# Chunk places laid out anew and a new TensorE order in the mixers of a two-layer mixer and mixture-of-experts step on one core

## What is computed

```python
for l in range(2):
    sh1, sc1, g1, sh2, sc2, g2 = split(silu(cond) @ w_ada[l] + b_ada[l], 6)   # per group of tokens
    h = rms_norm(x, norm1_g[l]) * (1 + sc1) + sh1
    z = h @ w_in[l]                       # 1024 -> 2048 mixer columns + 4 * 1024 gate logits
    # four mixers on the 2048 columns: conv (31 taps, layer norm, silu), Fourier,
    # windowed attention with rotary embedding and sinks, 2-D neighbourhood attention
    proj = einsum('blnc,ncd->blnd', branches, w_branch[l])
    merged = einsum('blnd,blnd->bld', sigmoid(gate_logits), proj)
    x = x + g1 * (merged @ w_out[l])
    h = rms_norm(x, norm2_g[l]) * (1 + sc2) + sh2
    aff = softmax(h @ w_router[l])        # 16 experts; each takes its top tokens (16 prompt, 32 sample)
    x = x + g2 * scatter_add(expert_swiglu(h[idx]) * g)
y = rms_norm(x, final_norm_g)
```

## Time and profile before

| what | us |
|---|---|
| median of 3 runs | 1682.55 (1682.27 to 1686.41) |
| the profiled execution's own time | 1680.36 |
| its span | 1678.5 |
| TensorE matmuls busy | 1558.4 (93%) |
| DVE, ACT, POOL busy | 522.1, 493.8, 358.9 |
| DMA | 536.72 MB, mean 320 GB/s |

### The profile page before, as it was taken

One profiled execution on the slowest core, in us unless ns is written; L12 is line 12 of the kernel. 1 busy time (PEld: TensorE's weight loads), 2 busy tenths in 40 slices (PEclk: granted clock), 3 DMA queues, 4 the chain that ended last, 5 costly groups with the idle time before them and its releaser, 6 DMA issues.

```text
span 1678.5 us, 20053 instructions
## 1 busy us (share of the span) xinstructions
PE 1558.4 (93%) x8363; PEld 955.6 (57%) x8363; DVE 522.1 (31%) x864; ACT 493.8 (29%) x910; POOL 358.9 (21%) x196
## 2 busy tenths in 40 slices
PE   7999999999999998799799999999999998988986
PEld 4988889984333343242279888899733433423322
DVE  3733453533121121121157234445411211212013
ACT  4435454433112021121153455534321211211212
POOL 1544455730000000000035444558000000000000
PEclk9999999999999999999999999999999999999999
DMA  9624444479999999999994434445799999999995
GB/s 377 243 100 152 160 151 151 149 304 418 428 426 426 427 426 427 427 428 428 421 392 158 138 124 151 151 158 221 327 422 426 428 426 428 427 426 428 426 427 237
DMA packets 52098, 536.72 MB, mean 320 GB/s; under 512 B 13584, under 2 KB 13992, under 8 KB 20008
## 3 DMA queue, kind: packets, MB, share of 16 engines
q1 hardware_dynamic: 52008, 535.43, 77.7%
HBM read 533.05 MB, written 2.36 MB: 319 GB/s over the span
## 4 chain that ended last, share of the span: by engine, by line
PE 68%; DMA 22%; ACT 4%; DVE 3%; issue 1%; POOL 1%; SPq 0%; DVEq 0%; ACTq 0%
PE psum L967 22%; PE psum L1771 17%; DMA ring<-in_w_e_down 11%; PE psum L1800 8%; DMA ring<-in_w_e_gu 8%; PE psum L1200 4%; PE psum L1130 3%; PE psum L1739 3%; PE psum L1817 2%; PE psum L707 2%; DMA ring<-in_w_in 1%; DMA ring<-in_w_ada 1%; PE psum L1103 1%; PE psum L1082 1%; ACT WSR L1220 1%
## 5 line engine op out<-in xcount | busy, mean ns | idle before, releaser
L967 PE MATMUL psum<-HTH,WSR 128*128 128x384 f32 x1536 | 412.3, 342 | 1.8 <-ACT arena L630 1.6
L1771 PE MATMUL psum<-ring,arena 128*64 128x512 f32 x1504 | 339.7, 596 | 27.9 <-DMA ring<-in_w_e_gu 26.6
L967 PEld LDWEIGHTS psum<-HTH,WSR 128*128 128x128 f32 x1536 | 280.4, 188 | 14.9 <-issue 11.8
L899 POOL TENSOR_TENSOR WSR<-ring,WSR 128x1024 fp32r<-128x1024 f32 x92 | 224.0, 2434 | 252.5 <-ACT WSR L1220 252.5
L967 PE MATMUL psum<-HTL,WSR 128*128 128x384 f32 x768 | 259.4, 338 | 0.0
L1771 PEld LDWEIGHTS psum<-ring,arena 128*64 128x64 f32 x1504 | 103.5, 137 | 232.8 <-issue 186.7
L1948 DVE TENSOR_TENSOR arena<-arena,psum 64x512 f32<-64x512 f32 x64 | 44.1, 690 | 503.1 <-PE psum L1771 315.0
L1800 PE MATMUL psum<-ring,arena 128*64 128x512 f32 x864 | 193.5, 595 | 5.2 <-DMA ring<-in_w_e_down 5.2
L1220 ACT ACTIVATE WSR<-ring 128x1024 fp32r<-128x1024 f32 x96 | 101.6, 1059 | 281.8 <-PE psum L967 279.4
L967 PEld LDWEIGHTS psum<-HTL,WSR 128*128 128x128 f32 x768 | 144.8, 189 | 1.0 <-issue 1.0
L1854 ACT ACTIVATE arena<-psum 64x512 f32<-64x512 f32 x64 | 37.7, 589 | 347.9 <-PE psum L1771 347.7
(11 more groups left out here) (221 smaller groups left out, 1695.1 us busy)
## 6 DMA issues: line engine op xcount, KB each, us to landing
ring<-in_w_e_gu SPq DMA_DIRECT2D x94, 2048.0 KB, 31.2
ring<-in_w_e_down SPq DMA_DIRECT2D x54, 2048.0 KB, 31.4
ring<-in_w_ada SPq DMA_DIRECT2D x24, 2048.0 KB, 10.7
ring<-in_w_in SPq DMA_DIRECT2D x22, 2048.0 KB, 7.9
arena<-in_w_e_gu SPq DMA_DIRECT2D x22, 1536.0 KB, 29.1
arena<-in_w_e_gu SPq DMA_DIRECT2D x12, 2048.0 KB, 29.5
arena<-in_w_e_down SPq DMA_DIRECT2D x10, 2048.0 KB, 31.4
C<-in_w_e_gu SPq DMA_DIRECT2D x22, 512.0 KB, 30.8
```

What stands on the lines that cost most here:

```text
L899: nc.gpsimd.tensor_tensor(WSR[:, 1, i % 2], part_src(i), WSR[:, 0, i % 2].bitcast(F32), ALU.subtract).then_inc(S["w_rest"], 1)
L967: ins = nc.tensor.matmul(ps[:, 0:TOK], WSR[:, w, i % 2, k, :], x[:, k, :], start=(k == 0 and w == 0 and x is HTH), stop=(k == KT - 1 and w ...
L1771: ins = nc.tensor.matmul(pb[half][64 * m:64 * m + 64, :], XE[:, k, j, :], w[:, half * CH:(half + 1) * CH], start=(k == 0), stop=(k == KT - 1))
```

## The change

1. **Mixer order.** fa2 comes behind the projection cq1. rot0 and rot1 come behind dq0, rotk behind zcv, lt0 and lt1 behind that, lt2 behind dk0, lb0 and lb1 behind dv0, ko behind dv1. vt0 to vt2 come inside gate step 0, behind its gate tile. ACT's order follows, with the square root behind the copy of dk1.
2. **Modulation.** ADA_AT changes from {0: 4, 4: 5, 8: 6, 11: 7, 20: 8, 24: 9} to {2: 4, 5: 5, 8: 6, 11: 7, 14: 8, 17: 9, 20: 10}: chunk 10 is multiplied at step 20 and kept in bank 4 until the routing. Chunk 11 is multiplied where chunk 10 was, behind the last logits. ada4, 8, 9 and 10 are loaded into slot 6.
3. **Places.** The order is now 4, 0 (after w_branch), LOW, HIGH, 1, 6, 2, 3, 5. Chunk 0 is fetched when the last attention output is copied. Chunk 9 (ONCE) has a place of its own, half in GROW, half in once_slot, used once a layer. The chunks after it turn through the nine places as before.
4. **What makes room.** The split of the merged rows (MRGH) moves from ring slot 4 to XN, laid out by token tile; the last branch's rest (BRL_LAST) to ring slot 5; an expert's transposed activations from AT into XE; one square's output into the arena.
5. **Banks.** wo{t}_{half} has bank (t + 3 half) mod 4; rt{t} keeps bank t; ada10 has bank 4.

```diff
-        ADA_AT = {0: 4, 4: 5, 8: 6, 11: 7, 20: 8, 24: 9}
+        ADA_AT = {2: 4, 5: 5, 8: 6, 11: 7, 14: 8, 17: 9, 20: 10}
...
-                 "w5", "ada7", "w8", "wb23", "w9", "ada8", "w10", "ada9", "w11", "wo0", "wo1", "ada10", "ada11"]
+                 "w5", "ada8", "ada7", "w8", "wb23", "ada9", "w9", "w10", "ada10", "w11", "wo0", "wo1", "ada11"]
...
-        MRGH = over("MRGH", "ring", 4 * 4 * D, KT * TOK)[:, :].rearrange("p (k t) -> p k t", k=KT)
+        MRGH = over("MRGH", "XN", 0, KT * TOK)[:, :].rearrange("p (t k n) -> p k t n", t=TT, k=KT)
...
-                T.add(f"wo{t}_{half}", 2 * t + half)
+                T.add(f"wo{t}_{half}", (t + half * TT) % 4)
...
-            PLACE = (LOW, HIGH, unit_at["wo0"][0], SPARE, unit_at["wo1"][0], 3, 4, unit_at["ada10"][0], unit_at["ada11"][0])
+            third = 3 - unit_at["wo0"][0] - unit_at["wo1"][0]
+            PLACE = (4, third, LOW, HIGH, unit_at["wo0"][0], SPARE, unit_at["wo1"][0], 3, unit_at["ada11"][0])
             RING = len(PLACE)
+            ONCE = RING
+            def turn(x):
+                return x if x < ONCE else x - 1
...
-                s, landing = PLACE[x % RING], e_land[x % RING]
+                if x == ONCE:
+                    sp.dma_start(GROW[:, 0].rearrange("p i d -> p (i d)"), src[:, 0:2 * D]).then_inc(once_land, 16)
+                    sp.dma_start(once_slot, src[:, 2 * D:4 * D]).then_inc(once_land, 16)
+                    return
+                s, landing = PLACE[turn(x) % RING], e_land[turn(x) % RING]
...
+                    if s == 4:
+                        copied(sp, f"o{len(ATT) - 1}")
...
+                    elif name == "w11":
+                        first_chunk(0)
                     elif name == "wo1":
-                        first_chunk(0)
-                sp.wait_ge(S["out_kv"], base("out_kv") + 64)
-                for x in range(1, RING - 1):
+                        first_chunk(1)
+                        sp.wait_ge(S["out_kv"], base("out_kv") + 64)
+                        first_chunk(2)
+                for x in range(3, RING - 1):
                     first_chunk(x)
...
                 used_up(sp, "ada11")
                 fetch(sp, RING - 1, chunk(l, (RING - 1) // PER, (RING - 1) % PER))
+                sp.wait_ge(S["x_mixed"], base("x_mixed") + 2 * TT)
+                sp.wait_ge(S["router_exp"], base("router_exp") + 1)
+                fetch(sp, ONCE, chunk(l, ONCE // PER, ONCE % PER))
...
-                for x in range(RING, NE * PER):
-                    used_place_of(x - RING)
+                for x in range(ONCE + 1, NE * PER):
+                    used_place_of(x - RING - 1 if x < 2 * RING + 1 else x - RING)
...
-                ada_main(pe, l, 10)
+                ada_main(pe, l, 11)
```

More of the change, by code:

```diff
@@ L976, in mixer_tensor, with channel_dft @@
                     copied(pe, f"zf{c}")
-                for t in range(TT):
+                def channel_dft(t):
                     ps = open_tile(pe, f"fa{t}")
@@ new lines, in rotated, with conv_rows @@
+                def rotated(n, src):
+                    ps = open_tile(pe, n)
+                    close_tile(nc.tensor.matmul(ps[:, 0:DEC], rot, src, start=True, stop=True), n)
+                def conv_rows(t):
+                    ps = open_tile(pe, f"lt{t}")
+                    a0 = 0 if t == 0 else USAMP - PADC + (t - 1) * P
+                    for c in range(2):
+                        ins = nc.tensor.transpose(ps[:, c * P:(c + 1) * P], ACC[:, c, a0:a0 + P], ident)
+                    close_tile(ins, f"lt{t}")
@@ new lines, in normed_back, with prompt_keys @@
+                def normed_back(c):
+                    ps = open_tile(pe, f"lb{c}")
+                    for t in range(TT):
+                        ins = nc.tensor.transpose(ps[:, t * P:(t + 1) * P], LNX[:, t, c * P:(c + 1) * P], ident)
+                    close_tile(ins, f"lb{c}")
+                def prompt_keys():
+                    ps = open_tile(pe, "ko")
+                    for n in ("cq0", "cq1", "ck", "dk0", "dk1"):
+                        copied(pe, n)
+                    for c, src in enumerate((KTC[:, 0:P], DK[:, 0, 0:P], DK[:, 1, 0:P])):
+                        ins = nc.tensor.transpose(ps[:, c * P:(c + 1) * P], src, ident)
+                    close_tile(ins, "ko")
@@ L983, in mixer_tensor, with value_rows @@
+                def value_rows(t):
+                    ps = open_tile(pe, f"vt{t}")
+                    for c in range(3):
+                        ins = nc.tensor.transpose(ps[:, c * P:(c + 1) * P], VT[:, c, t * P:(t + 1) * P], ident)
+                    close_tile(ins, f"vt{t}")
+                channel_dft(0)
+                channel_dft(1)
                 zt("cq1")
+                channel_dft(2)
                 ps = open_tile(pe, "ctxT")
@@ L1044, in att_scores @@
+                zt("dk0")
+                conv_rows(2)
+                zt("dk1")
+                zt("dv0")
+                for t in range(TT):
+                    copied(pe, f"lt{t}")
+                for c in range(2):
+                    normed_back(c)
+                zt("dv1")
+                prompt_keys()
                 def att_scores(g):
@@ L1118, in mixer_tensor @@
                         zt(f"g{n}_{k}")
+                        if idx == 0:
+                            for x in ("zcv", "dv0", "dv1"):
+                                copied(pe, x)
+                            for t in range(TT):
+                                value_rows(t)
                         if go is not None:
@@ L1331, in mixer_scalar @@
                     if idx == 0:
-                        for c in range(2):
-                            ps = take(act, f"lb{c}")
-                            release(nc.scalar.activation(BRT[:, 0, c, :], ps[:, 0:TOK], ACT.Silu, scale=PRM[:, 128 + c:129 + c],
-                                                         bias=PRM[:, 130 + c:131 + c]), f"lb{c}")
+                        for t in range(TT):
+                            copy_out(f"vt{t}", ZV[:, t, :], lambda ps: ps[:, 0:384])
                     if go is not None:
```

181 lines of the change are left out of this document (86 added, 95 removed).

## The result

The changed kernel took 1677.05 us (median of 10 runs, 1669.57 to 1680.45), the kernel before 1684.95 in the runs beside it. The ratio is **0.9947, interval 0.9929 to 0.9965**: 0.5% faster, by the ratio 8.9 us, where 23 were forecast. The profiled execution took 1675.76 us (span 1674.0), 4.6 less than that of before.

A forecast was written before the change was run, and what follows sets the result against it. TensorE was taken to bound the mixer and the DMA stream the experts. Places -6.4 and order -5.1 gave -11.5 us a layer, -23.0 for two, hence 1659 us; forecast 1653 to 1665, range with rivals 1650 to 1670.

The forecast's parts named there:

- Order ahead of step 7: TensorE's reordered mixer up to step 7's gate tile: forecast 6.5 us less a layer.
- -0.9: Channel DFT: a projection now covers the third tile's 0.92 us wait for ACT, 0.9 us less a layer.
- -3.8: Mixer transposes put between projections: -4.4 us, plus 0.6 for a new wait, so 3.8 us less a layer.
- the softmax wait of 1.78: Attention: TensorE's wait for the first scores' softmax goes, covered by moved modulation chunk 4.
- The new wait for the normalised rows: Behind dv0, TensorE waits for rows scaled after ACT's square root: +0.6 us, between 0 and 2.
- Chunk 10's +1.9 less the second softmax wait: Modulation chunk 10 added to the attention steps costs 1.9 us; the fifth scores' 1.49 us wait goes.
- w4: w_in piece loaded one step later, some 3.5 us after ACT wants it; covered, so 0, up to 3.5 us.
- rival (b): Order gains nothing: late w4, square root and ACT's table loads eat it; only the places count, 1670 us, chance 0.12.
- The logits on the last w_out tile's bank: Routing: tile 1's logits wait for DVE to empty the bank shared with the last w_out tile, +1.0 us.
- The places: Expert chunks: more loaded early and chunk 9's own place end the stream 6.4 us earlier a layer, bounds 4.9 to 8.1.
- the lag of 1.4 us: Start lag of the emptied DMA engines, read at one start; used for restarts instead of the skill's 2.0.
- The clock: Rival: TensorE stays at 1.2 GHz over a whole first expert group, 1817 us, chance 0.03; short dip 1.7 a layer.

The follow-up runs named there:

- c2: b3 with modulation chunk 4 multiplied at step 0 again, as in the kernel before: 1662.34 us, ratio 0.9863 to the kernel before.
- a1: Changed kernel with modulation chunk 5 multiplied at step 4 instead of 5, so w4 loads earlier: 1666.93 us, ratio 0.9888 to the kernel before.
- a4: Changed kernel with the chunk places of the kernel before, leaving the new order alone: 1687.86 us, ratio 1.0013 to the kernel before.
- b1: Changed kernel without the place used once; chunk 9 takes the first ring place again: 1683.65 us, ratio 1.0005 to the kernel before.
- a3: Changed kernel with chunk 5 at step 4 and tile 1's logits in PSUM bank 5: 1663.87 us, ratio 0.9869 to the kernel before.
- b3: b2 with two of six groups of logits moved into w_out tiles: 1658.59 us, ratio 0.9852 to the kernel before.
- a2: Changed kernel with the logits of tile 1 in PSUM bank 5 instead of bank 1: 1672.20 us, ratio 0.9917 to the kernel before.
- b2: a3 plus three idle products, matmuls nobody reads, where TensorE waits for DVE ahead of the experts: 1659.74 us, ratio 0.9857 to the kernel before.
- b4: b2 plus two idle products between the groups of logits, on the path: 1660.99 us, ratio 0.9865 to the kernel before.
- c1: b3 with the normalised rows' transposes behind dv1, their wait left ahead of it: 1659.81 us, ratio 0.9841 to the kernel before.
- c3: b3 on the chunk places of the kernel before: 1670.37 us, ratio 0.9907 to the kernel before.
- c4: b3 with dv1 ahead of TensorE's wait for the scaled rows as well as the transposes: 1657.09 us, ratio 0.9844 to the kernel before.

## Why the prediction was wrong

The sign was right, the size was not: 1659 forecast, 1677 measured, outside the range of 1650 to 1670. By the steps of the prediction:

- **Order ahead of step 7: right.** -0.9, -3.8 and the softmax wait of 1.78 are -6.5, and layer 1 has -6.5: 5.0 up to step 0, 1.5 from there to step 7. The terms -0.9 and -3.8 weren't tried one by one. The new wait for the normalised rows was 0.8 to 0.9 us for the 0.6 forecast. Chunk 10's +1.9 less the second softmax wait gave +0.4, as forecast. c2 shows that chunk 4 covers the softmax.
- **w4: the step that failed.** The prediction said: "its split on POOL is needed only two projections later; and the branch product of step 7 has about 0.9 us to spare. I count 0, up to 3.5." The delay was sized well: ACT wants w4 when step 6's gate tile is done, at 165.8, and starts on it at 169.60, 3.8 us late for the 3.5 forecast. The cover was wrong. I looked at who reads w4's parts. What counts is what stands behind w4's copy in ACT's program: the sigmoid of another tile, with a PSUM bank that TensorE needs one step later. The slack of two tiles is worth nothing to it. It cost 3.1 to 3.4 us a layer and the low clock behind it another 1.5; a1 takes both away and gets 10 us. The sign set for it, a wait of TensorE for POOL at steps 7 to 9, named the wrong engine, too: the wait was for ACT. The upper end of the term, 3.5, stood in rival (b); as the likely value it gives 1666 by itself.
- **The logits on the last w_out tile's bank: right**, +0.95 for +1.0.
- **The places: right in kind, about 1 us a layer short.** 6.4 forecast, 5.6 by the ratio of a4, within the bounds of 4.9 to 8.1. By 416.5 the changed kernel had moved 354 GB/s x 40.4 us = 14.3 MB since 376.13; the forecast had 7 chunks, 14.7 MB: 0.9 us late, so the restarts behind the first releases cost more than the lag of 1.4 us taken for them. The same shows in the ten traces with all the new places: from a layer's first expert product to the next layer's first projection, or to the end, they are 3.7 to 5.9 us shorter than before, just under 5 in the mean, and never 6.4. The 5.8 a layer that follows from the Trainium skill's fixed cost of a DMA (SBUF — State Buffer, "The DMA setup-cost knee") was the nearer number; whether the lag has that cause no run here shows. That the place used once is worth one chunk's time was the model's point, and b1's 4.9 a layer agrees with it.
- **The clock: seen as a rival, sized wrongly.** I let it decide only from a low level of 60 us on and priced a short fall at 1.7 us a layer, without counting that there can be several. The profiled run lost 1.5 and 1.6 us behind step 7, and in the second routing 5 us, which is the 6.0 of the table less the bank's 1.0. "The same gaps gave no dip at 376 to 391" took one execution for a rule, while the mean clocks of the kernel before range from 0.987 to 0.998. The routing had been stripped of a chunk of 16 products, had a new wait, and then fell to 1.2 GHz in some executions and not in others. The Trainium skill's warning of gaps between bursts (TensorE: Matmul & The Clock Gate, "Why this matters for your kernels") fits the fall behind the 3.26 us at step 7, and six of the seven other places of that wait. It does not cover a3, where TensorE had no such gap ahead of the fall, only a row of very small products.

Of the 18.4 us between the forecast gain of 23 and the 4.6 of the profiled runs, w4's wait is 6.5, the low clock behind it 3.1, the low clock in the second routing 5.0, the places 3.2 and the opening 0.6; the rest is rounding. A check from the other side: b3, with w4, the bank and the routing's clock mended, has a profiled execution at before's mean clock of 0.997, and its span is 22.1 us shorter than before's.

Which feature of the routing decides on the clock stays open in part. These are the stretches at 1.2 GHz between the last w_out tile and the experts, over all traces with the new order:

| kernels | layers | layers with such a stretch |
|---|---|---|
| 24 small products in a row, no products in the waits (changed kernel, a1, a2, a3, a4, b1) | 12 | 10 |
| idle products in the waits (b2) | 2 | 1 |
| these and two between the logits (b4) | 2 | 0 |
| these and the logits spread (b3, c1, c2, c3, c4) | 10 | 0 |

The runs agree: the mean clocks of the first group lie between 0.986 and 0.995, b2's and b4's between 0.995 and 0.997, and 21 of the 23 of the last group at 0.996 or more. So idle products and spread logits together take the fall away, and a2 and a3 show that it doesn't need the wait of the logits. How much of this the spreading does isn't shown, since no kernel here has it without the idle products and b3 is hardly fuller than b2. The fall in the opening, in ten of these thirteen traces, wasn't tried.

## What to carry to other kernels

When a load is issued later, look past its readers: ask what stands behind the first waiting instruction on that in-order engine, and which buffers those later instructions free. When work is moved out of a thin stretch, see whether small products and waits are what is left, and look at the granted clock there in more than one execution; a wait that exists anyway can be filled at no cost. And check in the trace that the edit did what its name says; a ratio that hits the expectation, as c1's did, is no proof.

## What the runs showed of the hardware

TensorE fell to 1.2 GHz for stretches of only 3.4 to 10.2 us, and some 0.4 us were lost for each us there. It isn't the same from one execution of a kernel to the next: the ten runs' mean clocks range from 0.987 to 0.994 and their times by 11 us along with them. In a3 it fell without any wait ahead of it, behind 24 products of 16 columns; behind idle times of 2.9 to 3.5 us it fell in seven of eight places. Three restarts of the emptied DMA engines cost about 1 us more in all than three times the lag of 1.4 us read at one start.
